# The last output quadrant of a Strassen-Winograd down projection: added by VectorE and stored by the sync engine, where GpSimd's adding transfers did it

## What is computed

```python
x = x + g1 * mix
h2 = modulate(rms_norm(x, norm_ffn_w[l]), sh2, sc2)
up = depthwise_conv(h2 @ w_up[l], ffn_conv_w[l], ffn_conv_b[l])
gate, val = jnp.split(up, 2, axis=-1)
x = x + g2 * ((jax.nn.silu(gate) * val) @ w_down[l])
```

## Time and profile before

| | |
|---|---|
| median of 3 runs | 1194.03 us (1193.31 to 1195.86) |
| span of the profiled execution | 1198.3 us |
| its TensorE busy share | 95% |
| its VectorE busy share | 78% |
| its ScalarE busy share | 48% |
| its GpSimd busy share | 24% |

### The profile page before, as it was taken

How to read it: one execution, slowest core, us unless ns; L and a number is a source line. 1 busy time by engine, 2 the same in 40 slices (tenths; PEclk the granted TensorE clock), 3 DMA queues, 4 the chain that set the end, 5 groups by cost and what they waited for, 6 DMA issues and landing times.

```text
span 1198.3 us, 17077 instructions
## 1 busy us (share of the span) xinstructions
PE 1135.2 (95%) x5953; PEld 964.9 (81%) x5953; DVE 935.2 (78%) x1426; ACT 575.3 (48%) x983; POOL 291.1 (24%) x331
## 2 busy tenths in 40 slices
PE   6899999989999999998799999999999999999996
PEld 6877788889898887786688878787878878888885
DVE  3269988769897664459999999999999875867763
ACT  4352346756565765555444434343434444444441
POOL 2100011115454100002545454455410020000111
PEclk9899999989998999999899999999999999999999
DMA  9321555619999414213445454545433284443474
GB/s 368 133 76 61 127 106 108 122 54 233 251 261 258 141 53 158 106 64 94 139 147 169 142 169 129 175 127 184 130 119 105 89 285 171 115 115 97 119 164 70
DMA packets 103090, 171.77 MB, mean 143 GB/s; under 512 B 9322, under 2 KB 62690, under 8 KB 102004
## 3 DMA queue, kind: packets, MB, share of 16 engines
q1 hardware_dynamic: 82388, 104.70, 26.5%
q0 software_dynamic: 20640, 66.27, 23.4%
HBM read 112.21 MB, written 31.46 MB: 120 GB/s over the span
## 4 chain that ended last, share of the span: by engine, by line
PE 39%; DVE 13%; issue 6%; ACT 5%; DVEq 0%; ACTq 0%; POOL 0%
PE ps L1610 16%; PE ps L1660 6%; PE ps L1661 6%; PE ps L1662 6%; PE ps L1575 5%; DVE y L2026 3%; DVE w_op L1927 3%; DVE w_raw L1945 2%; DVE y L2022 2%; ACT w_op L1731 1%; ACT y L1819 1%; DVE u L2015 1%; DVE s_sum L1945 1%; ACT h_second L1724 0%; PE ps L1586 0%
## 5 line engine op out<-in xcount | busy, mean ns | idle before, releaser
L1610 PE MATMUL ps<-t_op,w_op 128*128 128x512 f32 x1056 | 248.1, 390 | 3.8 <-DVE cv L2015 1.7
L1610 PEld LDWEIGHTS ps<-t_op,w_op 128*128 128x128 f32 x1056 | 197.2, 188 | 49.1 <-issue 6.3
L1610 PE MATMUL ps<-hx,w_op 128*128 128x512 f32 x792 | 191.5, 395 | 9.7 <-DVE u L2015 7.0
L1610 PEld LDWEIGHTS ps<-hx,w_op 128*128 128x128 f32 x792 | 150.5, 191 | 43.6 <-DVE u L2015 6.5
L1731 ACT ACTIVATE w_op<-w_raw 128x512 fp32r<-128x512 f32 x132 | 79.9, 622 | 197.3 <-DVE w_raw L1945 184.6
L1660 PE MATMUL ps<-dnh,ah 128*128 128x512 f32 x308 | 120.1, 390 | 1.6 <-DVE dnl L2033 1.6
L1661 PE MATMUL ps<-dnl,ah 128*128 128x512 f32 x308 | 119.9, 389 | 0.0
L1662 PE MATMUL ps<-dnh,al 128*128 128x512 f32 x308 | 119.8, 389 | 0.0
L1927 DVE TENSOR_TENSOR w_op<-w_raw,w_op 128x512 fp32r<-128x512 f32 x132 | 100.6, 777 | 9.9 <-ACT w_op L1731 8.0
L1839 ACT ACTIVATE ah<-hid 128x512 fp32r<-128x512 f32 x77 | 48.6, 632 | 116.6 <-PE ps L1662 112.5
L2033 DVE TENSOR_TENSOR al<-hid,ah 128x512 fp32r<-128x512 f32 x77 | 53.2, 691 | 48.6 <-ACT ah L1839 47.8
(11 more groups left out here) (288 smaller groups left out, 2381.9 us busy)
## 6 DMA issues: line engine op xcount, KB each, us to landing
w_raw<-in_w_up SPq DMA_DIRECT2D x44, 512.0 KB, 5.1
wm<-in_w_mod SPq DMA_DIRECT2D x32, 512.0 KB, 6.3
sums<-wm POOLq DMA_DIRECT2D x32, 512.0 KB, 7.9
wd<-in_w_down POOLq DMA_DIRECT2D x44, 256.0 KB, 3.3
w_down_sums<-wd POOLq DMA_DIRECT2D x44, 256.0 KB, 2.8
dn_raw<-w_down_sums SPq DMA_DIRECT2D x44, 256.0 KB, 2.6
hid_scratch<-hid SPq DMA_DIRECT2D x20, 512.0 KB, 4.0
hid<-hid_scratch POOLq DMA_DIRECT2D x20, 512.0 KB, 5.8
```

What stands on the lines that cost most here:

```text
L1610: last = pe.matmul(bank_of(p, s), w_op[p][w][:, k, :], rows_of(p, k, v), start=(start and k == 0 and w == 0 and v == 0), stop=(k == KH - 1 ...
```

## The change

The lower left quadrant goes another way. During product 6, behind the load for step 22, the sync engine reads the quadrant's x1 back from `out` into the buffer `w21` (4 transfers, semaphore `kept_in`). `w21` (the product) is written into `u4_all`, in place, and a new VectorE operation `x21` adds it to the x1 that was read back. Behind `c21` a second new operation, `o21`, adds the last product, and the sync engine stores the result plainly. GpSimd's 8 adding transfers of `w21` and `c21` are gone, as is its wait between them; it now ends with the wait for the other 12, and the sync engine ends with a wait for its 4 loads and 4 stores.

```diff
-        QUAD_OPS += [(name, t) for t in range(4) for name in ("s22", "c22", "w21")]
-        QUAD_OPS += [(name, t) for t in range(4) for name in ("s12", "c12")] + [("c21", t) for t in range(4)]
+        QUAD_OPS += [(name, t) for t in range(4) for name in ("s22", "c22", "w21", "x21")]
+        QUAD_OPS += [(name, t) for t in range(4) for name in ("s12", "c12")] + [(name, t) for t in range(4) for name in ("c21", "o21")]
...
                 for n in range(4, NSTEP):
                     load_step(n)
+                    if n == 2 * NK2:
+                        sp.wait_ge(x1_out, 16 * TT)
+                        for t in range(TT // 2):
+                            r0 = (TT // 2 + t) * P
+                            sp.dma_start(w21[:, t, :], out[0, r0:r0 + P, 0:HALF]).then_inc(kept_in, 16)
+
+                for t in range(TT // 2):
+                    r0 = (TT // 2 + t) * P
+                    sp.wait_ge(quad_read, quad_at("o21", t))
+                    sp.dma_start(out[0, r0:r0 + P, 0:HALF], w21[:, t, :]).then_inc(kept_in, 16)
+                sp.wait_ge(kept_in, 16 * 8)
...
-                        ins = dve.tensor_tensor(out=w21[:, t, :], in0=u2_all[:, t, :], in1=g2[0], op=ALU.mult)
+                        ins = dve.tensor_tensor(out=u4_all[:, t, :], in0=u2_all[:, t, :], in1=g2[0], op=ALU.mult)
+                    elif name == "x21":
+                        dve.wait_ge(kept_in, 16 * 4)
+                        ins = dve.tensor_tensor(out=w21[:, t, :], in0=w21[:, t, :], in1=u4_all[:, t, :], op=ALU.add)
+                    elif name == "o21":
+                        ins = dve.tensor_tensor(out=w21[:, t, :], in0=w21[:, t, :], in1=p1_all[:, t, :], op=ALU.add)
...
                 for t in range(TT // 2):
                     quad("c21", t)
+                    quad("o21", t)
...
                     accumulate("c22", t, 1, 1, g22[:, t, :], stored)
-                    accumulate("w21", t, 1, 0, w21[:, t, :], w21_stored)
                 for t in range(TT // 2):
                     accumulate("c12", t, 0, 1, g12[:, t, :], stored)
-                pool.wait_ge(w21_stored, 16 * 4)
-                for t in range(TT // 2):
-                    accumulate("c21", t, 1, 0, p1_all[:, t, :], stored)
-                pool.wait_ge(stored, 16 * 16)
+                pool.wait_ge(stored, 16 * 12)
```

More of the change, by code:

```diff
@@ L1427, in build @@
             back_in = [sem4(f"back_in{i}") for i in range(NXT)]
-            dn_sum, dn_hi, dn_split, dn_mm, bank_mm, p1_copied, quad_read, stored, w21_stored = (
-                sem4(n) for n in ("dn_sum", "dn_hi", "dn_split", "dn_mm", "bank_mm", "p1_copied", "quad_read", "stored", "w21_stored"))
+            dn_sum, dn_hi, dn_split, dn_mm, bank_mm, p1_copied, quad_read, stored, kept_in = (
+                sem4(n) for n in ("dn_sum", "dn_hi", "dn_split", "dn_mm", "bank_mm", "p1_copied", "quad_read", "stored", "kept_in"))
             block = s4.enter_context(nc.Block())
@@ L2153, in _ @@
                     if i in (1, 3, 5, 7):
-                        for name in {6: ("c11",), 5: ("u2",), 7: ("u4",), 3: ("s22", "c22", "w21"), 4: ("s12", "c12")}.get(p, ()):
+                        for name in {6: ("c11",), 5: ("u2",), 7: ("u4",), 3: ("s22", "c22", "w21", "x21"), 4: ("s12", "c12")}.get(p, ()):
                             quad(name, i // 2)
```

## The result

The changed kernel takes 1184.19 us (median of 5 runs, 1180.81 to 1189.59), the kernel before 1193.31 in the same comparison (5 runs, 1189.08 to 1195.86). The ratio is 0.9925, 95% interval 0.9898 to 0.9953. A second comparison on one chip, with 29 runs of the kernel before (median 1193.08) and 6 of the changed one (1184.75), gives 0.9941, interval 0.9921 to 0.9961.

A forecast was written before the change was run, and what follows sets the result against it. TensorE was taken to bound the down projection, leaving gains behind the last matmul: drain 4.6, landing 2.2, issue 0.6, less 0.96 for `o21`, make 6.4 us. From the median 1194.03 that gives 1187.6 us, range 1186.3 to 1192.4.

The forecast's parts named there:

- What bounds the kernel: Down projection: TensorE's matmuls set the pace, busy 30.00 of 30.00 us; the change can win only behind the last matmul.
- The mechanism of the end: Behind the last matmul: 11.3 us, 10.5 of it GpSimd's transfer, drain and semaphores; VectorE and a plain store replace them.
- GpSimd's drain: At the block's end: the drain of 4.63 us leaves the path, over before the store has landed; saves 4.6 us.
- landing: Last transfer to HBM: a plain store lands in 2.6 us where the adding transfer took 4.8; saves 2.2 us.
- issue: Between VectorE's last operation and the last transfer: the sync engine issues after 0.05 us instead of 0.67; saves 0.6 us.
- `o21`: End of VectorE's work: one more operation per tile makes a chain of eight, ending 0.96 us later than before.
- `x21` costs nothing: Product 3: four more VectorE operations, 0.72 us each, are covered by the splits' lead; without cover 2.9 us.
- The read-back costs nothing: Step 22: four 256 KB loads delay step 23's weights to 6.3 us, wanted after 9.4; uncovered about 3.7 us.
- The missing drain: Rival at the block's end: plain runs lack the drain, so only 1.8 us are won, 1192.2 us; chance 0.17.
- Slow stores: Rival at the last store: writing 2 KB rows to HBM, not adding, took 4.8 us; 1189.8 us, chance 0.06.
- starving: Rival at step 23: the read-back delays the weights TensorE needs, making the kernel slower, 1196.4 us; chance 0.03.
- How the numbers follow: Closing step: forecast's chance 0.74, time 1187.6 us, own range 1186.3 to 1189.2, widened to 1192.4 for the missing drain.

The follow-up runs named there:

- drain_back: The changed kernel, but GpSimd also waits for the sync engine's four stores before its drain; median 1190.39 us (12 runs), ratio to before 0.9985.

## Why the prediction was wrong, point by point

**What bounds the kernel: right.** TensorE's pace through the down projection is untouched. Three stretches of the changed kernel, from ahead of the read-back (1014.65) to the last matmul (busy time, PE first):

```profile
1010.00:1036.00 26.00, 26.00 (x116) 21.52 (x116) 23.61 (x38) 11.11 (x20) 1.73 (x2) 1.00 0.55 153
1036.00:1106.00 70.00, 70.00 (x311) 57.97 (x310) 51.97 (x82) 30.02 (x52) 1.68 (x2) 1.00 0.41 108
1106.00:1178.00 72.00, 72.00 (x319) 59.45 (x317) 52.47 (x83) 27.73 (x48) 6.71 (x8) 1.00 0.48 111
```

**The mechanism of the end: right in every piece.** Of the sizes, the landing was the one off. The terms, each as before less after:

| term | predicted | measured |
|---|---|---|
| GpSimd's drain | 4.6 | 4.6 |
| landing | 2.2 (4.8 - 2.6) | 2.8 (4.8 - 2.0) |
| issue | 0.6 | 0.6 |
| `o21` | -0.96 | -1.0 |
| the end | 6.4 | 7.0 |

`o21` ended 1.80 behind the last matmul, where 1.76 was worked out. The landing was taken from a store of twice the bytes (2.6), with the remark that half should not take longer; it took 2.0. It had been read as the cost at hand, not as the upper bound that the remark made it. The statement that no plain store of 256 KB is in the trace is also wrong. GpSimd stores the weight sums to HBM with 44 of them, in the DMA issues of the kernel before:

```profile
w_down_sums<-wd POOLq DMA_DIRECT2D x44, 256.0 KB, 2.8
```

Their 2.8 us, beside other traffic, would not have given the 2.0, and would have made the term smaller still. But they come from GpSimd and don't add, so they spoke before any run for the adding, and against the rival that the write itself takes 4.8.

**`x21` costs nothing: right.** The first round of product 3 in the changed kernel, and ScalarE's row that marks TensorE's arrival at step 57, as in the earlier trace rows:

```profile
1120.25 0.69 DVE L2141 TENSOR_TENSOR u_all<-u_all,g2b 128x512 f32<-128x512 f32 x1
1120.97 0.69 DVE L2144 TENSOR_TENSOR w<-w,u_all 128x512 f32<-128x512 f32 x1
1121.58 0.69 DVE L2044 TENSOR_TENSOR al<-hid,ah 128x512 fp32r<-128x512 f32 x1
1122.18 0.68 DVE L2044 TENSOR_TENSOR dnl<-dn_raw,dnh 128x512 fp32r<-128x512 f32 x1
```

```profile
1123.81 0.63 ACT L1850 ACTIVATE ah<-hid 128x512 fp32r<-128x512 f32 x1 [1.56 <-PE ps L1673]
```

The split is done at 1122.86 (1122.18 + 0.68), and TensorE wants it at 1123.81: a lead of 0.95, forecast 0.96.

**The read-back costs nothing: right.** The sync engine around step 22, and the landings of the four reads and of the two loads around them (the last row of the timeline merges the loads for steps 23 and 24):

```profile
1014.28 0.33 SPq L1554 DMA_DIRECT2D dn_raw<-w_down_sums  x1
1014.65 1.85 SPq L1568 DMA_DIRECT2D w<-out_latent  x4
1017.00 3.05 SPq L1554 DMA_DIRECT2D dn_raw<-w_down_sums  x2
```

```profile
w<-out_latent SPq DMA_DIRECT2D x4, 256.0 KB, 4.2
dn_raw<-w_down_sums SPq DMA_DIRECT2D x2, 256.0 KB, 3.8
```

The reads issue at 0.43 each rather than 0.33, still in time: the load for step 23 goes out 2.72 behind that for step 22, as before. The two loads land after 3.8 us in the mean (2.5 for step 22 and 5.0 for step 23, where 6.3 was worked out), against the 9.4 that step 23's may take, and TensorE's lead of 8.82 us at this place is the same at the last matmul: it lost nothing in between.

**The rivals.** The missing drain fell: `drain_back` shows the drain in the time. It rested on the span being 4.3 us over the median, and that was a comparison of different executions. In each run that has both, time and span are 1.7 to 1.9 us apart, the time being the longer (1184.19 and 1182.4). The Trainium skill's rule (Runtime: NRT & Kernel Launch, section The ~15µs preamble/postamble breakdown), that the profile's total is the longer one by some 6 us, is not borne out for the span here. Slow stores and starving fell with the rows above: the store landed in 2.0 us, and TensorE was busy without a gap.

**The steps that failed are two.** The first is a term of the sum, the landing: 2.6 us were taken for the store, and it took 2.0. The second, and the larger, is the last one, "How the numbers follow". It took the median of three runs as the fixed point (the 29 later runs have 1193.08, 0.95 lower), and made the low end of the range from the store's bound alone, with nothing for the spread of single runs; the 1189.2 of its upper end is worked out from no row. The later median and the measured end together give 1193.08 - 7.04 = 1186.0, already 0.3 below the range. The remaining 1.8 to the measured 1184.19 is within the spread of five runs that lie 8.8 us apart; which way the median of five falls in it is chance. The low end should have stood some 3 us lower. The share of the gain, 0.54% forecast, is inside the measured interval of 0.47 to 1.02%, near its lower end, and inside that of the second comparison, 0.39 to 0.79%.

## What to carry to other kernels

Read the rows behind the last landing, not only the chain up to it: an engine's drain can stand on the path with all work done, and it is hidden by giving the last transfers to an engine whose drain is short, while GpSimd's runs earlier. The two edits pay together: the addition on chip without the change of issuer left the end at 10.3 of 11.3 us, and only moving the wait to the sync engine, without the addition, left it at 9.8; the addition with the sync engine's stores made 4.2. And when a kernel's runs spread by 1%, in part with the granted clock, the range of a predicted time must hold that spread, however sure each term is; the end behind the last matmul, which was 4.24 us in each of four profiles, is the better place to test the terms.

## What the hardware showed that was not expected

- GpSimd's drain at the end of a block took 4.63 to 5.45 us in eight profiles with all its transfers landed, and 8.17 to 14.19 where it started with one in flight, over 2.6 to 2.9 us behind that one's landing. The number of transfers at the end (8 to 24) and the time since its last one (up to 16.8 us) made no difference beyond that. The sync engine's took 0.12 us at most.
- A plain store of 256 KB landed in 2.0 us from the sync engine and 2.3 from GpSimd; an adding transfer of the same bytes took 4.8 among others of its kind, and 4.1 in the median where they were issued 4.3 us or more apart.
- At identical instructions, two executions stood 8.8 us apart ahead of the down projection, of which about 8 go with how long TensorE was granted the lower of its two clocks (some 44 against 28 us).
